# Shared expert: gate and up products on centered, weighted rows; deviation and shift applied to the products

## The reference, cut to what matters

```python
x = layer_norm(ALPHA * x + m @ w_o, ln1_g, ln1_b)      # (x - mean) * rsqrt(var + eps) * g + b
scores = sigmoid(x @ w_router)                         # 264 x 64, then 8 experts for each token
shared = (silu(x @ ws_gate) * (x @ ws_up)) @ ws_down   # 1024 -> 256 -> 1024
routed = sum over the 8 experts of weight * ((silu(x @ w_gate[e]) * (x @ w_up[e])) @ w_down[e])
x = layer_norm(ALPHA * x + routed + shared, ln2_g, ln2_b)
```

## Time and profile before

| | |
|---|---|
| median of 3 runs | 836.07 us |
| the profiled execution | 835.78 us, span 834.0 us |
| front part, to the last strip | 0 to 318.3 us |
| middle part, to the first expert pair | 318.3 to 348.08 us |
| 32 expert visits | 348.08 to 817.2 us |
| end: last sums, second norm, store | 817.2 to 834.0 us |
| a visit of two experts | 14.50 us, in the last turn 15.3 to 16.4 us |
| TensorE busy | 815.8 us (98%) |
| VectorE, ScalarE, GpSimd busy | 506.8, 195.1, 93.0 us |
| moved by DMA | 262.03 MB |

### The profile page before, as it was taken

How to read it: one execution, slowest core, us unless ns; L and a number is a source line. 1 busy time by engine, 2 the same in 40 slices (tenths; PEclk the granted TensorE clock), 3 DMA queues, 4 the chain that set the end, 5 groups by cost and what they waited for, 6 DMA issues and landing times.

```text
span 834.0 us, 12706 instructions
## 1 busy us (share of the span) xinstructions
PE 815.8 (98%) x4523; PEld 501.9 (60%) x4523; DVE 506.8 (61%) x1212; ACT 195.1 (23%) x300; POOL 93.0 (11%) x104
## 2 busy tenths in 40 slices
PE   8999999999999999899999999999999999999994
PEld 7876788877788888544545444454544444455452
DVE  6989899999741367635545454554545455454566
ACT  2210011112121005322222222222232322222225
POOL 1029700000010002100000000000000000000021
PEclk9999999999999999999999999999999999999998
DMA  9433344445599946599999999999999999999971
GB/s 336 142 129 101 125 152 146 142 140 107 146 353 419 394 152 256 196 388 416 419 420 417 420 421 420 419 421 420 421 419 421 420 419 421 420 418 420 419 299 52
DMA packets 50548, 262.03 MB, mean 314 GB/s; under 512 B 10504, under 2 KB 11272, under 8 KB 25296
## 3 DMA queue, kind: packets, MB, share of 16 engines
q1 hardware_dynamic: 45904, 252.88, 76.8%
q0 software_dynamic: 4608, 8.66, 2.8%
HBM read 267.10 MB, written 2.53 MB: 323 GB/s over the span
## 4 chain that ended last, share of the span: by engine, by line
PE 94%; DVE 2%; DMA 2%; ACT 1%; issue 1%; SPq 0%; ACTq 0%; DVEq 0%
PE banks L1206 33%; PE banks L1408 26%; PE banks L1448 14%; PE banks L1381 11%; PE banks L1356 3%; DMA ring<-w_front 2%; PE banks L1310 1%; PE banks L1221 1%; PE banks L1233 1%; PE banks L1386 1%; PE banks L1423 1%; PE banks L1474 0%; ACT cgb L682 0%; PE banks L1316 0%; PE banks L1291 0%
## 5 line engine op out<-in xcount | busy, mean ns | idle before, releaser
L1408 PE MATMUL banks<-high,low 128*64 128x512 f32 x848 | 225.1, 592 | 0.1
L1206 PE MATMUL banks<-xT,ring 128*128 128x264 f32 x768 | 177.0, 389 | 1.1 <-DMA ring<-w_front 1.1
L1206 PEld LDWEIGHTS banks<-xT,ring 128*128 128x128 f32 x768 | 143.9, 190 | 32.5 <-issue 6.8
L1408 PEld LDWEIGHTS banks<-high,low 128*64 128x64 f32 x848 | 72.3, 137 | 145.4 <-issue 145.4
L1116 DVE TENSOR_TENSOR cgb<-cgb,banks 128x264 f32<-128x264 f32 x248 | 90.1, 424 | 49.9 <-PE banks L1381 49.9
L1161 DVE SCALAR_TENSOR_TENSOR high<-banks,sml,low 128x1024 f32<-128x1024 f32 x31 | 39.8, 1284 | 122.3 <-ACT low L670 122.3
L1381 PE MATMUL banks<-xT,low 128*128 128x264 bf16 x744 | 92.6, 277 | 0.0
L1381 PEld LDWEIGHTS banks<-xT,low 128*128 128x128 bf16 x744 | 66.1, 98 | 42.0 <-issue 24.3
L516 POOL DMA_INDIRECT low<-x_rows_dram,idx x32 | 31.9, 997 | 429.6 <-DVE idx L1061 425.1
L1408 PE MATMUL banks<-ring,low 128*64 128x512 f32 x176 | 77.4, 593 | 0.0
L1448 PE MATMUL banks<-high,mu 128*64 128x512 f32 x336 | 76.7, 598 | 0.2 <-DVE cgb L1116 0.2
(11 more groups left out here) (295 smaller groups left out, 926.4 us busy)
## 6 DMA issues: line engine op xcount, KB each, us to landing
high<-w_gu SPq DMA_DIRECT2D x108, 1024.0 KB, 23.8
high<-w_dn SPq DMA_DIRECT2D x42, 1024.0 KB, 23.1
ring<-w_front SPq DMA_DIRECT2D x78, 512.0 KB, 3.3
ring<-w_gu SPq DMA_DIRECT2D x22, 1024.0 KB, 24.9
us<-w_dn SPq DMA_DIRECT2D x11, 1024.0 KB, 23.5
bgb<-w_dn SPq DMA_DIRECT2D x6, 1024.0 KB, 21.0
xcb<-w_dn SPq DMA_DIRECT2D x5, 1024.0 KB, 21.6
xT<-x_t SPq DMA_DIRECT2D x4, 264.0 KB, 4.0
```

What stands on the lines that cost most here:

```text
L1206: ins = pe.matmul(psum[:, 6 + n % 2, 0:T], ring[:, n % RING, k], rhs[:, k], start=(k == 0), stop=(k == KC - 1))
L1408: ins = pe.matmul(psum[SL * j:SL * j + SL, GU_BANK, :], xg[:, k, SL * j:SL * j + SL], gu[slots[j]][:, k], start=(k == 0), stop=(k == KC - 1))
```

## The change

- The shared expert's gate and up products read `r_` times the norm's weight instead of x1. The weight is multiplied into `r_` in place, six chunks by VectorE (`DVE_ROWS`) and two by ScalarE. The deviation (per token) is multiplied onto the four products afterwards. The norm's shift becomes one more column: `xcb` is 265 wide, its last column holds the shift, and the product of that column is added as a bias, in ScalarE's silu or in VectorE's last multiplication (`scale_shared`).
- x1 is now the weighted row times the deviation. VectorE makes four chunks (`DVE_X1`), GpSimd the other four. ScalarE adds the shift as before.
- The logits' eight steps come in one block ahead of the squares, since the rows are overwritten. GpSimd adds five squares instead of four, TensorE four instead of five in all.
- TensorE starts the shared products before the scores, without the six warming matmuls. All three token blocks of x1 are turned in one block. Shared products are cut differently over the pauses. Banks are reassigned.
- On SP's queue both halves of slot 3 are loaded together when all shared products are made, and `dn[7]`, whose buffer the shared products now read, comes behind them.

```diff
-        xcb = sb("xcb", [P, KC, T])
+        xcb_wide = sb("xcb", [P, KC, T + 1])
+        xcb = xcb_wide[:, :, 0:T]
...
@@ sync
-                sp.wait_ge(x1_scaled, KC)
-                sp.dma_start(dn[7], w_dn[6]).then_inc(dn_in[7], 16)
                 for c in range(TC):
                     sp.wait_ge(xrow_ready, c + 1)
                     sp.dma_start(x_dram[c * P:c * P + tok[c]], xrow[c][0:tok[c]]).then_inc(rows_stored, 16)
-                sp.wait_ge(shared_mid, 1)
                 sp.wait_ge(gathered[0], 16)
-                load_gu(3, w_gu[5], [0])
                 sp.wait_ge(shared_gu, 2 * FC)
-                load_gu(3, w_gu[5], [1])
+                load_gu(3, w_gu[5])
+                sp.wait_ge(x1_scaled, DVE_X1)
+                sp.wait_ge(x1_scaled_pool, KC - DVE_X1)
+                sp.dma_start(dn[7], w_dn[6]).then_inc(dn_in[7], 16)
@@ gpsimd
+                pool.wait_ge(rows_weighted, DVE_ROWS)
+                pool.wait_ge(rows_weighted_act, KC - DVE_ROWS)
+                pool.wait_ge(deviation_ready, 1)
+                for n in range(DVE_X1, KC):
+                    pool.tensor_tensor(x1[:, n], r_[:, n], mu[:, 0], ALU.mult).then_inc(x1_scaled_pool, 1)
@@ scalar
+                    if nth == 0:
+                        for n in range(DVE_ROWS, KC):
+                            act.wait_ge(squared, n + 1)
+                            act.wait_ge(logits_done, n + 1)
+                            act.activation(r_[:, n], r_[:, n], ACT.Copy, scale=vec[:, V_LN + n:V_LN + n + 1]).then_inc(rows_weighted_act, 1)
...
                 for f in range(FC):
-                    act.wait_ge(shared_gu, f + 1)
-                    act.activation(sil[:, f], psum[:, SHARED_BANKS[f], 0:T], ACT.Silu).then_inc(shared_silu, 1)
+                    act.wait_ge(gates_scaled, f + 1)
+                    act.activation(silu_in[f], silu_in[f], ACT.Silu, bias=shared_shift[:, f:f + 1]).then_inc(shared_silu, 1)
@@ vector
+                for k in range(DVE_ROWS):
+                    dve.wait_ge(squared, k + 1)
+                    dve.wait_ge(logits_done, k + 1)
+                    dve.tensor_scalar(r_[:, k], r_[:, k], vec[:, V_LN + k:V_LN + k + 1], None, ALU.mult).then_inc(rows_weighted, 1)
                 deviation(0)
+                dve.sem_inc(deviation_ready, 1)
...
-                for n in range(KC):
-                    dve.scalar_tensor_tensor(x1[:, n], r_[:, n], vec[:, V_LN + n:V_LN + n + 1], mu[:, 0], ALU.mult, ALU.mult).then_inc(x1_scaled, 1)
+                for n in range(DVE_X1):
+                    dve.tensor_tensor(x1[:, n], r_[:, n], mu[:, 0], ALU.mult).then_inc(x1_scaled, 1)
...
+                def scale_shared(f, out):
+                    dve.wait_ge(shared_gu, SHARED_ORDER.index(f) + 1)
+                    st.did(dve.tensor_copy(shared_shift[:, f:f + 1], psum[:, SHARED_BANKS[f], T:T + 1]))
+                    return dve.tensor_tensor(out, psum[:, SHARED_BANKS[f], 0:T], mu[:, 0], ALU.mult)
...
-                    dve.tensor_tensor(hT[:, f], sil[:, f], psum[:, SHARED_BANKS[FC + f], 0:T], ALU.mult).then_inc(shared_h, 1)
+                    dve.scalar_tensor_tensor(hT[:, f], hT[:, f], shared_shift[:, FC + f:FC + f + 1], silu_in[f], ALU.add, ALU.mult).then_inc(shared_h, 1)
@@ tensor
-                        ins = pe.matmul(psum[:, SHARED_BANKS[f], 0:T], gu[3][:, k, f * P:f * P + P], x1[:, k], start=(k == 0), stop=(k == KC - 1))
+                        ins = pe.matmul(psum[:, SHARED_BANKS[f], 0:T + 1], gu[3][:, k, f * P:f * P + P], xcb_wide[:, k], start=(k == 0), stop=(k == KC - 1))
...
-                keep_warm(6, 2)
-                turn_scores()
+                shared_pair(0, 3)
+                turn_scores()
+                shared_pair(3, 5)
```

## The result

The changed kernel took 839.02 us (median of 6 runs, 838.39 to 841.42), the kernel before 836.02 beside it: a ratio of 1.0042, 95% interval 1.0032 to 1.0052. Measured again later (e16) it was 840.63 against 835.96, ratio 1.0056 (1.0043 to 1.0070). The forecast was 837.4 with a range of 834.9 to 839.5. The sign was right, and the measured time lies inside the range; the size was less than half: +1.33 us forecast, +3.00 measured. The profiled execution took 838.39 us with a span of 836.6, 2.6 us more than the one before.

What follows compares the result with a forecast made beforehand. Transfers were taken as the slower side, 1.7 us of slack behind TensorE's first visit. The stream 3.15 us later less 1.7 slack gave +1.45 us: 837.2 or 837.5 by base, forecast 837.4, range 834.9 to 839.5.

Steps and rivals of the forecast that it cites:

- What bounds the kernel: Steady visits: transfers are the slower side; TensorE's first visit and the stream of loads are limits 1.7 us apart.
- Ahead of the deviation: Before the deviation: logits ahead of the squares, less one square product, make it 0.5 us later; contention may add 0.2.
- The 0.2 us for contention: VectorE's six weight multiplications against GpSimd's last two square additions: 0 to 0.6 us, taken as 0.2.
- x1: VectorE's four x1 chunks alternate with GpSimd's four: 3.2 us instead of 3.33, -0.1 us for the router.
- The rival in which GpSimd holds VectorE off: At x1, VectorE waits until GpSimd's four multiplications are through, 4.3 us: 838.7 us in all, chance 0.12.
- The router's list: TensorE's turns and nine shared products after the scores' reading take 7.1 us, hidden by 0.4 under the router's 7.5.
- The first visit: TensorE's first visit after the weight selection: starts 0.35 us earlier, from +0.6, -0.5 and -0.45.
- half a microsecond back at the selection: At the first selection: three shared products stand before it instead of four, so 0.5 us comes back.
- three products behind the weights instead of four: Between weight selection and first visit: one shared product less, a gain of 0.45 us.
- The loads: SP's queue: 5.0 us of moved transfers, 1.5 recovered, so the stream comes 3.5 us later at an unmoved first visit.
- The forecast waits of 1 to 3 us in the last turn: Sign of being right: TensorE waits on w_gu transfers, first in last-turn visits, some 1 to 3 us in all.
- Shared expert behind that: After the shared products: VectorE's copies, multiplications and ScalarE's work fit within the first visit and cost nothing.

Runs made afterwards that it cites:

- e16: The changed kernel as it is, measured again on the same chip as e15: 840.63 us, ratio 1.0056 to the kernel before.
- e15: The changed kernel with eight short unit-matrix products, then TensorE's two register reads, ahead of the wait for the gathered rows: 837.64 us, ratio 1.0024.
- e4: The changed kernel with all eight weight multiplications on ScalarE, none on VectorE: 838.38 us, ratio 1.0028 to the kernel before.
- e6: The changed kernel with four squares added on GpSimd instead of five (three additions): 839.63 us, ratio 1.0040 to the kernel before.
- e9: e8 with the kernel before's order around the squares (logits split, three GpSimd additions, four rows weighted by VectorE): 835.70 us, ratio 0.9994.
- e13: e9 with short unit-matrix products filling TensorE's three gaps around the gathered rows: 836.82 us, ratio 1.0006 to the kernel before.
- e3: The changed kernel with all eight x1 multiplications on VectorE, none on GpSimd: 838.01 us, ratio 1.0026 to the kernel before.
- e1: The changed kernel with eight short unit-matrix products where TensorE idles before the gathered rows: 838.00 us, ratio 1.0026 to the kernel before.
- e2: The kernel before with only SP's queue order changed as in the change (slot 3, then dn[7], after the shared products): 837.16 us, ratio 1.0016.
- e12: The changed kernel with only TensorE's two register reads moved ahead of the wait for the gathered rows: 837.99 us, ratio 1.0032 to the kernel before.
- e5: The changed kernel with the last three shared products moved ahead of the wait for the gathered rows: 838.67 us, ratio 1.0037 to the kernel before.
- e10: The kernel before with only TensorE's two register reads moved ahead of the wait for the gathered rows: 835.55 us, ratio 0.9993.
- e7: The changed kernel with the edits of both e5 and e6: 840.48 us, ratio 1.0052 to the kernel before.
- e8: e5 with TensorE's two register reads also moved ahead of the wait for the gathered rows: 835.72 us, ratio 0.9996 to the kernel before.
- e11: e9 with the weight multiplications of the rows taken out of the deviation's way: 836.31 us, ratio 1.0002 to the kernel before.

## Why the forecast was half the size, step by step

*What bounds the kernel: right.* Two limits close together, TensorE's first visit and the stream of loads. e15 and e16 show it best: 3.4 us more on the one make 1.3 us of waits for the other vanish. The chain of the changed kernel went by TensorE's start, though, where the forecast's sum went by the stream.

*Ahead of the deviation: +0.7 forecast, 1.62 - 0.36 = +1.26 measured.* The 0.2 us for contention fit (0.18, e4). What was missing is the 0.52 us by which the fourth addition stood behind the third, with VectorE busy (the changed kernel) or not (e4); what they are is open. Taking that addition away didn't help (e6), since the weight multiplications, costed at 0.27 us each in idle time, took 0.45 us each and in e6 0.58; in e9 four of them took 0.8 us each, in e13 0.4.

*x1: right.* 3.2 us forecast, 2.95 measured, alternating with GpSimd, and e3 shows that VectorE alone is as fast. The Trainium skill (SBUF — State Buffer, section "SBUF: two separate sides") has the two engines exclude each other for a whole instruction when VectorE's has two inputs in SBUF and GpSimd's reads SBUF; these rows agree, with 0.74 and 0.81 us an instruction against 0.355 (2.84 / 8) alone. The rival in which GpSimd holds VectorE off had 838.7 us, nearer to the result than the forecast, but not its 4.3 us for x1: its number is not what happened. (By its own terms its first visit is at 2.1 - 0.5 - 0.45 = +1.15 and not +0.9.)

*The router's list: nearly right.* Scores read +1.56, counts at 337.80 against 336.12, +1.68. The forecast had TensorE's list end 0.4 us ahead of the picks. The list started 0.74 us behind the reading, when the scores had been copied (330.89 against 330.15), and ended at 337.76, the picks' last cast at 337.64: it cost 0.1 us instead of nothing.

*The first visit: the step that failed.* Forecast -0.35, measured +1.66, and +2.24 at the second visit. The text had the router 0.6 us later, half a microsecond back at the selection, and three products behind the weights instead of four as a gain of 0.45 us. The half microsecond came back (counts 1.32 us later than before once the fronts are level, the last cast 0.89), but from a router 1.2 us late instead of 0.6, and the 0.45 us became a loss. The text didn't ask what TensorE has left to do when the gathered rows come. The shared products start earlier now, the gather later, and 3 of 32 products were held back behind the weights: TensorE ran dry at 343.1 and the clock fell. The low clock added 0.98 us to the three products (2.57 - 1.59) and 0.58 to the first visit (13.55 us to the second instead of 12.97). But without it the register reads would have stood there, so the experiments give the split of the 2.24 us, by the second visit's distance from the mean's matmul: 0.36 are the front part's, 46.95 - 45.92 = 1.03 the fall of the clock (against e1), 45.92 - 45.33 = 0.59 the register reads (e1 against e15), and 45.33 - 45.07 = 0.26 the later router less what the shorter list gave back (e15 against the kernel before). Each of these is read from one profile. In e16, where the fall was twice as long, it costs 48.28 - 45.92 = 2.36 us.

*The loads: mechanism right, size smaller.* With the first visit 0.2 us later the stream came 2.5 us later (e2), where 3.5 was forecast at an unmoved one (1.8 to 4.7): of the 5.0 us of moved transfers about 2.7 were recovered, where 1.5 was forecast. The wait is 0.98 us in e2; forecast for it was 3.5 - 1.7 = 1.8. In the changed kernel it was 0.30 us, or none (e16), since TensorE itself came late. The forecast waits of 1 to 3 us in the last turn didn't show there; without the fall they are 0.72 us (e1), 1.29 (e15) and 1.32 (e12).

*Shared expert behind that: right.* VectorE's four scalings and two last multiplications began at 350.2 and were over at 353.4; nothing waited for them.

The number 837.4 was thus near what the change costs when neither the clock falls nor the register reads hold up the first visit: e15 is that kernel, 837.64 us, its first visit 0.25 us later than before once the fronts are level and its waits 1.29 us. With the gap filled alone (e1) it is 838.00. Part of that nearness is luck: the router was later and the stream earlier than forecast.

## What to carry to other kernels

When work is moved ahead in a hand-written order, list what the engine has left at each wait behind it, not only what stands on the path: an engine that runs dry pays with its wait, and TensorE may pay again with its clock. Work that was filler before (here the products behind the weights, which also hid register reads) must be looked at for what it covered. With two limits close together, a gain or loss on one is read only after the other has been put level, as e15 against e16.

## What the runs showed of the hardware that was not expected

- Two reads of a number from SBUF into TensorE's registers, with their operations and bounds checks, hold its queue for 1.6 us (346.44 to 348.05 before, 347.62 to 349.26 in e5). Beside matmuls that are already in the queue they cost next to nothing: 0.2 us at the first visit of the kernel before (e10).
- After an idle time of 1.97 to 2.20 us and a second one of 0.6 to 0.9 us TensorE's granted clock fell to 1.2 GHz in the profiles of the changed kernel, e4, e6 and e16, for 3.4 us (the changed kernel, e4) or 6.8 to 6.9 (e6, e16); after 2.05 and 2.08 us in e3 and e12 it didn't. In e5, e7, e8 and e11, with shorter gaps of 0.4 to 0.9 us (and in e5 and e7 a further one of 1.45 and 1.41), it fell as well, in e9 not. The same kernel thus fell for 3.4 us in one execution and for 6.8 in another (e16), and one profile doesn't settle whether a gap costs anything.
- VectorE's in-place row products, 0.27 us each alone, took 0.8 us each beside GpSimd's additions, number fills and clearings in the profile of e9, and 0.4 us each beside the same work in that of e13.
